# Stick-breaking attention in a two-block transformer kernel: the cumulated sums as two single-pass products of softplus, split into a rounded half and a remainder

## The reference, cut to what matters

```python
def stick_breaking_attention(q, k, v):
    """q, k, v: (B, S, H, D). A[t,s] = beta_ts * prod_{s<j<t}(1 - beta_tj), s < t."""
    ...
        z = jnp.einsum('bqhd,bkhd->bhqk', qb, k).astype(jnp.float32) * scale
        mask = (k_pos[None, :] < q_pos[:, None])[None, None]
        log_1mb = jnp.where(mask, jax.nn.log_sigmoid(-z), 0.0)
        rem = lax.cumsum(log_1mb, axis=3, reverse=True) - log_1mb
        a = jnp.where(mask, jnp.exp(jax.nn.log_sigmoid(z) + rem), 0.0)
        return jnp.einsum('bhqk,bkhd->bqhd', a.astype(v.dtype), v)
```

## Time and profile before

| | |
|---|---|
| time, median of 3 runs | 2158.87 us (2158.61 to 2159.27) |
| the profiled execution, its own time | 2159.96 us |
| its span, first to last instruction | 2157.9 us |
| TensorE busy | 2049.3 us (95%) |
| VectorE busy | 864.5 us (40%) |
| ScalarE busy | 457.0 us (21%) |
| GpSimd busy | 359.8 us (17%) |
| mean granted TensorE clock | 0.977 of full speed |
| stick attention | about 1642.5 to 1726 us of the span |

### The profile page before, as it was taken

One profiled execution on the slowest core, in us unless ns is written; L12 is line 12 of the kernel. 1 busy time (PEld: TensorE's weight loads), 2 busy tenths in 40 slices (PEclk: granted clock), 3 DMA queues, 4 the chain that ended last, 5 costly groups with the idle time before them and its releaser, 6 DMA issues.

```text
span 2157.9 us, 41878 instructions
## 1 busy us (share of the span) xinstructions
PE 2049.3 (95%) x17400; PEld 1239.2 (57%) x17400; DVE 864.5 (40%) x1471; ACT 457.0 (21%) x740; POOL 359.8 (17%) x389
## 2 busy tenths in 40 slices
PE   6999898699999999999999999979998998999998
PEld 5888667243443443344343343337776787888887
DVE  4454435423333333332332332333665443544444
ACT  4251433000000000000000000024445422212211
POOL 1010000122223222232222222231201300000000
PEclk9999999799999999999999999979999999999999
DMA  6334113999999999999999999963111021232231
GB/s 238 110 118 140 59 40 114 402 392 403 406 410 404 403 411 406 402 408 404 400 403 405 402 406 399 400 233 108 59 59 39 1 78 59 90 104 97 81 112 41
DMA packets 157312, 520.48 MB, mean 241 GB/s; under 512 B 16412, under 2 KB 71760, under 8 KB 124400
## 3 DMA queue, kind: packets, MB, share of 16 engines
q1 hardware_dynamic: 136480, 494.96, 58.5%
q0 software_dynamic: 20784, 24.85, 4.8%
HBM read 509.61 MB, written 18.88 MB: 245 GB/s over the span
## 4 chain that ended last, share of the span: by engine, by line
PE 78%; DMA 7%; SPq 6%; DVE 4%; ACT 2%; issue 2%; POOL 1%; DVEq 0%; ACTq 0%; POOLq 0%
PE ps L2007 24%; PE ps L392 12%; PE ps L394 12%; PE ps L393 12%; PE ps L2021 11%; DMA ring_a<-in_w_gate_up 4%; SPq L567 3%; DMA ring_a<-in_w_down 3%; SPq L569 2%; PE ps L1900 1%; PE ps L494 1%; POOL rstd L466 1%; PE ps L1754 1%; PE ps L1910 1%; PE ps L1892 1%
## 5 line engine op out<-in xcount | busy, mean ns | idle before, releaser
L2007 PE MATMUL ps<-ring_a,xe 128*32 128x512 f32 x3912 | 436.6, 596 | 13.4 <-DVE xe L1602 9.1
L2021 PE MATMUL ps<-ring_a,act_t 128*32 128x256 f32 x6000 | 333.1, 379 | 6.0 <-DMA ring_a<-in_w_down 4.1
L2007 PEld LDWEIGHTS ps<-ring_a,xe 128*32 128x32 f32 x3912 | 124.8, 110 | 298.8 <-issue 257.2
L2021 PEld LDWEIGHTS ps<-ring_a,act_t 128*32 128x32 f32 x6000 | 193.0, 110 | 153.7 <-issue 21.4
L2007 PE MATMUL ps<-ring_b,xe 128*32 128x512 f32 x2232 | 251.8, 594 | 0.0
L392 PE MATMUL ps<-xt_hi,hi 128*128 128x512 f32 x576 | 228.7, 397 | 5.6 <-DVE xt_lo L507 4.7
L394 PE MATMUL ps<-xt_hi,lo 128*128 128x512 f32 x576 | 226.6, 393 | 0.0
L393 PE MATMUL ps<-xt_lo,hi 128*128 128x512 f32 x576 | 226.2, 393 | 0.0
L1089 ACT ACTIVATE glu<-glu 128x768 f32<-128x768 f32 x32 | 27.0, 843 | 649.7 <-DVE glu L1609 649.7
L759 POOL DMA_INDIRECT x_rows<-ye,idx x96 | 154.3, 1607 | 37.8 <-issue 37.8
L2007 PEld LDWEIGHTS ps<-ring_b,xe 128*32 128x32 f32 x2232 | 68.8, 110 | 150.6 <-issue 144.3
(11 more groups left out here) (296 smaller groups left out, 2413.9 us busy)
## 6 DMA issues: line engine op xcount, KB each, us to landing
ring_a<-in_w_gate_up SPq DMA_DIRECT2D x163, 1024.0 KB, 21.6
ring_a<-in_w_down SPq DMA_DIRECT2D x125, 1024.0 KB, 23.8
ring_b<-in_w_gate_up SPq DMA_DIRECT2D x93, 1024.0 KB, 20.0
raw<-in_w_in SPq DMA_DIRECT2D x20, 1024.0 KB, 7.7
raw<-in_w_gate SPq DMA_DIRECT2D x11, 1024.0 KB, 5.3
raw<-in_w_up SPq DMA_DIRECT2D x11, 1024.0 KB, 5.4
raw<-in_w_down SPq DMA_DIRECT2D x11, 1024.0 KB, 4.8
raw<-in_w_out SPq DMA_DIRECT2D x8, 1024.0 KB, 5.0
```

Source lines behind the costliest of these rows:

```text
L2007: last = pe.matmul(ps[QUAD * j:QUAD * j + QUAD, g, :], xe[:, g, QUAD * k:QUAD * k + QUAD], w[:, j, :, :, :], start=k == 0, stop=k == KT - 1)
L2021: last = pe.matmul(y_block(g, j), act_t[:, g, QUAD * (2 * c + h):QUAD * (2 * c + h) + QUAD], w[:, h, QF * j:QF * j + QF], start=c == 0 and ...
```

## The change

The cumulated sums are no longer ten float32 products but twenty float32r products of two parts of `sp`. After the mask, ScalarE copies `sp` tile by tile into a float32r tile `sp_hi` (`stick_hi`, which lies in the buffer of `z_e`), and VectorE subtracts it from `sp` into `sp_lo` (`stick_lo`, in place over `sp`). The constants of -1 are copied once into a float32r tile `tri`. On ScalarE the copies stand after a(h), ahead of out(h-1); on VectorE the subtractions stand at the end of the turn, ahead of abs(h+1). cum(h) now waits for `stick_lo` instead of the mask. softplus(h) waits for ln(h) tile by tile instead of for all of it. Two semaphores are made free elsewhere by using others in their place (`final_variance`, `lambda`), with the same waits.

```diff
+        sp_hi = at("sp_hi", HT, [P, 2, T, SEQ], F32R)
+        sp_lo = at("sp_lo", HT + 16 * KB, [P, 2, T, SEQ], F32R)
+        tri = at("tri", 120 * KB, [P, 2 * P], F32R)
...
-                    i = act.activation(z_e[:, h % 2, j, 0:w], z_e[:, h % 2, j, 0:w], ACT.Ln, bias=1.0)
-                i.then_inc(s_ln, 1)
+                    act.activation(z_e[:, h % 2, j, 0:w], z_e[:, h % 2, j, 0:w], ACT.Ln, bias=1.0).then_inc(s_ln, 1)
+
+            def stick_hi(h):
+                act.wait_ge(s_spm, h + 1)
+                for j in range(T):
+                    w = SEQ - P * j
+                    copy(sp_hi[:, h % 2, j, 0:w], sp[:, h % 2, j, 0:w]).then_inc(s_hi, 1)
...
+            copy(tri[:, :], const[:, C_NTRI:C_NTRI + 2 * P])
             stick_exp(0)
             stick_ln(0)
...
+            stick_hi(0)
             for h in range(SH):
                 if h + 1 < SH:
                     stick_exp(h + 1)
                     stick_ln(h + 1)
                 stick_a(h)
+                if h + 1 < SH:
+                    stick_hi(h + 1)
                 if h:
                     stick_out(h - 1)
...
             def stick_softplus(h):
-                dve.wait_ge(s_ln, h + 1)
                 if h >= 2:
                     dve.wait_ge(s_c, h - 1)
                 for j in range(T):
                     w = SEQ - P * j
+                    dve.wait_ge(s_ln, T * h + j + 1)
...
+            def stick_lo(h):
+                for j in range(T):
+                    w = SEQ - P * j
+                    dve.wait_ge(s_hi, T * h + j + 1)
+                    i = dve.tensor_tensor(sp_lo[:, h % 2, j, 0:w], sp[:, h % 2, j, 0:w], sp_hi[:, h % 2, j, 0:w].bitcast(F32),
+                                          ALU.subtract)
+                i.then_inc(s_lo, 1)
...
                 if h >= 4:
                     stick_scale(h - 4)
+                if h < SH:
+                    stick_lo(h)
...
-                pe.wait_ge(s_spm, h + 1)
+                pe.wait_ge(s_lo, h + 1)
                 for j in range(T):
                     for m in range(j, T):
-                        last = mm(stick_z(h, j)[:, (m - j) * P:], cc(C_NTRI if m == j else C_NONES),
-                                  sp[:, h % 2, m, 0:SEQ - m * P], start=False, stop=True, skip_group_check=True)
+                        for part_ in (sp_hi, sp_lo):
+                            last = mm(stick_z(h, j)[:, (m - j) * P:], tri[:, 0:P] if m == j else tri[:, P:2 * P],
+                                      part_[:, h % 2, m, 0:SEQ - m * P], start=False, stop=True, skip_group_check=True)
```

More of the change, by code:

```diff
@@ L333, in program @@
         x_set = sem("x_rows_set")
[L334 to L339, removed]
+        bd_done, comb, f_ss, f_rstd, f_x = (sem(f"final_{s}") for s in
+            ("bias", "sum", "squares", "rstd", "x"))
+        rel_dma, rel_flip, rel_f, rel_fs, lam_s, lam_e = (sem(f"rel_{s}") for s in
+            ("dma", "turned", "f", "f_sb", "lambda_sums", "lambda_exp"))
         hn_sq, hn_ss, hn_var, hn_rstd = (sem(f"head_norm_{s}") for s in ("squares", "sums", "variance", "rstd"))
@@ L347, in program @@
              "out", "out_evacuated"))
+        s_hi, s_lo = (sem(f"stick_{s}") for s in ("softplus_hi", "softplus_lo"))
         f_raw = [sem(f"f_raw_loaded{i}") for i in range(RAW)]
@@ L689, in final_rstd @@
                 pool.tensor_scalar(var[:, 50 + t:51 + t], ss[:, 50 + t:51 + t], 1.0 / D, EPS_1,
-                                   ALU.mult, ALU.add).then_inc(f_var, 1)
-                pool.wait_ge(f_var, t + 1)
+                                   ALU.mult, ALU.add).then_inc(mix_mean, 1)
+                pool.wait_ge(mix_mean, t + 2)
                 inverse_root(pool, rstd[:, 50 + t:51 + t], var[:, 50 + t:51 + t]).then_inc(f_rstd, 1)
@@ L1293, in vector_program @@
             link(dve.tensor_tensor(tiny[:, 44:45], tiny[:, 43:44], tiny[:, 42:43], ALU.subtract))
-            dve.tensor_scalar(tiny[:, 45:46], tiny[:, 44:45], LAMBDA_INIT, None, ALU.subtract).then_inc(lam_r, 1)
+            link(dve.tensor_scalar(tiny[:, 45:46], tiny[:, 44:45], LAMBDA_INIT, None, ALU.subtract))
             def combine(t):
@@ L1369, in scale_heads @@
                                   ALU.mult).then_inc(y_n, 1)
-            dve.wait_ge(lam_r, 1)
             diff_logits(0)
```

## The result

| | before | after |
|---|---|---|
| median of 9 executions each | 2159.27 us (2158.61 to 2162.68) | 2169.4 us (2164.97 to 2176.95) |
| ratio after to before | | 1.0046 [1.0034, 1.0057] |
| the profiled execution, its own time | 2159.96 us | 2167.87 us |
| its span | 2157.9 us | 2165.9 us |
| mean granted TensorE clock over its span | 0.977 | 0.972 |

A forecast was written before the change was run, and what follows sets the result against it. TensorE bounds heads 2 to 6 (9.06 us a head). Late start and new turns net +3.1, stretched masks +1.2: +4.3 on 2159.96 gives 2164.3, or 2163.2 as a median; range 2159.5 to 2168.5.

The forecast's parts named there:

- The sign: Whole kernel: slower, given 0.49, against 0.45 for the same and 0.06 for faster.
- the sum: Whole kernel: +3.1 net from start and turns, +1.2 for stretched masks, +4.3 us on the profiled execution.
- The new loop over ScalarE, GpSimd, VectorE, 8.63 a turn: Middle heads: each engine waits for the next within one turn, 8.63 us against 9.06 before.
- cum 2.75 us: Cumulated sums on TensorE: twenty float32r products take 2.75 us instead of 4.53 for ten float32 ones.
- Start: z(0) to a(1): subtractions delay VectorE, cum(1) at half clock takes about 4.4 us; a(1) 3.2 us later.
- Masks stretched, 1.2 in all: GpSimd masks beside VectorE's scalings from turn 4: 0.3 us more a turn, bounds nothing and 3.1 us.
- The root costs lo nothing: GpSimd's 1.01 us root beside VectorE's subtractions in the turn: does not lengthen them.
- rival C: Turns 2 to 7: subtractions wait for GpSimd's root, 0.75 us a turn, 4.5 in all; 2167.8 us, chance 0.14.
- TensorE is off this loop: Middle heads: cum ends 0.75 us ahead of need, so any cum up to 3.5 us is hidden.
- TensorE idles 1.3 us a turn: Middle heads, a sign of being right: TensorE stands idle 1.3 us in each turn.
- Rival D: Stick heads: TensorE stays at 1.2 GHz throughout, 11.4 us a turn; about 2176 us, chance 0.05.

The follow-up runs named there:

- experiment 3: Changed kernel plus TensorE products with unused results (128 rows) ahead of each cum, 8 in a middle head: 2163.4 us, 1.0016 against the kernel before.
- Experiment 1: Changed kernel with GpSimd's mask of sp(h+1) placed ahead of its mask of a(h): 2164.08 us, 1.0013 against the kernel before.
- experiment 7: Changed kernel with masks, root, sums, scalings and subtractions reordered: with filling products 2150.76 us, 0.9946 against the kernel before; without them 2157.87 us, 0.9996.
- experiment 2: Changed kernel without the subtractions and the remainder's products, cum being ten float32r products of sp_hi alone: 2174.78 us, 1.0064 against the kernel before.
- experiment 6: Changed kernel without subtractions and remainder's products, plus filling products: 2155.8 us (0.9975 against the kernel before) with 128 rows, 2197.18 us (1.0164) with 64.
- experiment 5: Changed kernel with mask sp(h+1) ahead of mask a(h) and filling products, three in a middle head: 2158.4 us, 0.9995 against the kernel before.
- experiment 4: Changed kernel with ten float32 products of the remainder alone in place of the twenty, copies, subtractions and waits kept: 2176.38 us, 1.0070 against the kernel before.
- e8: Changed kernel with the loop reordered, all computation kept, no filling products: 2157.87 us, 0.9996 against the kernel before.

## Why the prediction was wrong in size

The sign was right and the predicted 2163.2 us was 6.2 too low; the median lies 0.9 above the upper end of the range. Between the two profiled executions the excess over the sum is 3.7 us: 1.2 ahead of z(0), 1.0 in the start, 2.9 from a(1) to a(7) and 1.4 less behind it. The rest of the 6.2 comes from where these two executions lie among the others: the one before is 0.7 above its median of nine, the one after 1.5 below its own, and the median before moved up by 0.4. By the steps of the prediction:

- **The new loop over ScalarE, GpSimd, VectorE, 8.63 a turn.** Right: 8.64 in the first turn of after, each mark within 0.08 us, and 51.98 in all with the clock held up (experiment 3). Experiment 1 shows that the two masks ahead of hi are what makes it long.
- **cum 2.75 us.** Right at full clock: 2.71 on the chain of experiment 7.
- **Start.** lo(1) ends 22.8 us behind z(0), as said (1665.3 - 1642.52 = 22.8). cum(1) ran at half clock, as said, but took 5.35 us instead of 4.4: all twenty products were at that level, and their price there had been set too low. That is the 1.0.
- **Masks stretched, 1.2 in all.** Inside its bounds, but taken too high: 0.2 in each of two turns, 0.4 in all.
- **The root costs lo nothing.** Right, and rival C is out. The Trainium skill (SBUF — State Buffer, SBUF: two separate sides) would have lo wait for the root; the rows of the subtractions, at most 0.693 us beside a root of 1.01, do not agree.
- **"TensorE is off this loop: ... 0.75 us ahead of need, so any cum up to 3.5 us is hidden."** This is the step that failed. It holds at full clock only. At half clock cum takes 4.40 to 4.55, comes onto the loop, and the turn is 5.1 + 4.4 + 0.1 = 9.6: 0.9 and 1.1 more in the turns to a(3) and a(4). (These cums ran about 3 us at half clock and the rest at full; the 5.35 of cum(1) is what twenty products at half clock take.) In the last turn no slack hides anything: it takes 9.90 instead of 7.95, 1.8 of it from cum(7) at 4.54 and the rest from the masks. Together the three cums cost 3.8 us. The excess over the forecast from a(1) to a(7) is 2.9, since the masks took 0.8 less than forecast.
- **"TensorE idles 1.3 us a turn."** The idle time ahead of the middle cums is 0.62 to 1.23 us.
- **Rival D** was priced as all or nothing (2176 us, 0.05) and set aside with the clock's 1.00 through 3.4 us of idleness. That row says when the clock is still up, not what holds it up. Between "never" and "always" lies what happened: in both profiles cum(3), cum(4) and cum(7) out of the six behind cum(1), and by the mean clocks more half clock in other executions; where it lies in those was not profiled. The three slowest of the nine, at 2176.5 to 2177 us, lie at D's time, but that is luck. D's price took values at 2.3 us, and at half clock they take 4.27 (experiment 2). With 4.56 for z and 5.35 for cum a turn of D is 14.2 us, and an estimate of D from these rows is 2163.2 + 5 x (14.2 - 8.63) + (5.1 + 5.35 + 0.1 - 7.95), about 2194. So the slowest three are not D through and through. The Trainium skill (TensorE: Matmul & The Clock Gate, Why this matters for your kernels) too looks for such a drop in idle gaps between bursts. Experiment 2, and experiment 6 with 64 rows, do not agree that it takes a gap: the clock was 0.50 at 45.00 of 45.00 us busy.

Why the clock falls. Shown is that it does so in middle heads in both profiles of the changed kernel, and not in that of the kernel before. TensorE alone from a(1) to a(7), before:

```profile
1666.50:1717.70 51.20, 50.05 (x263) 1.00 0.00 1
```

Shown is also that filling products of 128 rows hold it up in the middle heads of the profiles of experiments 3, 5, 6 and 7, and that those of 64 rows do not (6). In the changed kernel two things came together: 1.8 us of full-height products went out of each head, while z (64 rows) and values (64 columns wide) stayed, so that the mixture shifted; and TensorE has idle time ahead of each cum, where in middle heads it had none. Experiment 2 shows that a mixture with still less full-height work is held at 0.50 with no idle time at all. But as to the changed kernel the profiles rather speak for the idle time: experiment 4 has the old kinds of product with 0.67 us of it, and the clock falls in cum(4); experiment 1 and e8 of experiment 7, both without filling, have the new mixture with at most 0.3 and 0.8 us ahead of a middle cum, and their clock is at 1.00 in all the middle heads. The length of the idle time alone does not decide either, since the clock fell behind 0.62 us (cum(4)) and not behind 1.23 (cum(6)). And of these two kernels no execution with a lower mean clock was profiled. So what share each of the two has in the changed kernel stays open. How z and values count, each by itself, was not tried.

## What to carry to other kernels

When a cheaper form of a step needs preparation on other engines, write down the whole loop of one turn with its queues before counting the freed engine's time: here 1.8 us of TensorE a head were traded for a loop that was itself 8.6 us long, and only putting the masks and sums into other slots made the saving arrive (7.7 a turn, experiment 7). Where dense products are thinned out between low or narrow ones, or idle time comes in between them, read the granted clock turn by turn and over several executions, and cost each step on the path at both levels. A spread of times that lies on a line with the mean clock is a reason to try a few filling products of full height.

## What the runs showed of the hardware that was not expected

- TensorE can be busy without a gap for 45 us and be granted 0.50 of its clock all the while (experiment 2, and experiment 6 with 64 rows).
- It can also fall to 0.50 behind as little as 0.62 to 1.03 us of idle time (cum(4) and cum(3) of the changed kernel), and not behind 1.23 us (cum(6)).
- Added products made a kernel 19 us faster when 128 rows high (2174.78 to 2155.8 us) and 22 us slower when 64 rows high (2197.18).
- At half clock the twenty float32r products of a cum (128 to 512 wide, with stationary operands of 128 columns) took 5.35 us against 2.71 at full clock, a factor of 1.97 on the chain. The values products, only 64 wide, went from 2.23 to 4.27.
- A GpSimd root of 1.01 us beside VectorE's subtractions of two SBUF inputs cost neither anything, while the GpSimd mask beside a scaling went from 0.63 to 0.81 and the scaling from 0.42 to 0.74.
